# ScalarE normalises half the columns of the first LayerNorm, copies the turned x before the high parts, and takes four copies of the second tokens

## What is computed

```
for i in range(DEPTH):                         # DEPTH = 2
    h = gated_short_conv(x, ...) if i == 0 else chunked_spatial_gating(x, ...)
    x = layer_norm(ALPHA * x + h, ln1_g[i], ln1_b[i])      # the first LayerNorm
    scores = sigmoid(x @ router_w[i])                      # 256 x 64
    # 4 of 8 groups by the sum of their two best scores, then 8 experts in them
    f = sum over the chosen experts: gate * (silu(x @ w_gate[e]) * (x @ w_up[e])) @ w_down[e]
        + the shared expert
    x = layer_norm(ALPHA * x + f, ln2_g[i], ln2_b[i])      # the second LayerNorm
```

## Time and profile before

| | |
|---|---|
| median of 3 runs | 1288.47 us |
| profiled execution, its own time | 1289.11 us |
| its span | 1287.3 us (1.81 us lie around it) |
| PE busy | 1205.8 us, 94% |
| DVE busy | 566.8 us, 44% |
| ACT busy | 376.9 us, 29% |
| POOL busy | 16.2 us, 1% |
| data moved by DMA | 473.87 MB, mean 368 GB/s |

### The profile page before, as it was taken

How to read it: one execution, slowest core, us unless ns; L and a number is a source line. 1 busy time by engine, 2 the same in 40 slices (tenths; PEclk the granted TensorE clock), 3 DMA queues, 4 the chain that set the end, 5 groups by cost and what they waited for, 6 DMA issues and landing times.

```text
span 1287.3 us, 20264 instructions
## 1 busy us (share of the span) xinstructions
PE 1205.8 (94%) x7896; PEld 732.6 (57%) x7896; DVE 566.8 (44%) x1264; ACT 376.9 (29%) x672; POOL 16.2 (1%) x32
## 2 busy tenths in 40 slices
PE   9999999999788888999999999999999898889897
PEld 7986444444234434559999998544444442444454
DVE  5756443333233223327676766634333332332233
ACT  4443221222022222315454444322222220222222
POOL 0001000000000000000000000000000000000000
PEclk9999999999889999999999999999999998999999
DMA  9977999999999999999735435899999999999996
GB/s 302 388 303 314 389 419 416 414 420 421 421 420 422 421 420 421 421 407 401 283 137 194 157 143 238 328 416 416 415 411 421 421 421 420 420 422 420 421 420 260
DMA packets 93937, 473.87 MB, mean 368 GB/s; under 512 B 8336, under 2 KB 23824, under 8 KB 48784
## 3 DMA queue, kind: packets, MB, share of 16 engines
q1 hardware_dynamic: 91776, 469.79, 90.1%
q10 hardware_dynamic: 2064, 2.75, 0.6%
HBM read 471.46 MB, written 1.05 MB: 367 GB/s over the span
## 4 chain that ended last, share of the span: by engine, by line
PE 64%; DMA 25%; SPq 5%; DVE 3%; issue 1%; ACT 1%; POOL 0%; DVEq 0%; ACTq 0%
DMA ring<-in_w_up 24%; PE ps L922 19%; PE ps L794 10%; PE ps L978 7%; PE ps L806 7%; PE ps L844 5%; PE ps L901 4%; PE ps L995 3%; SPq L495 3%; PE ps L934 2%; PE ps L1017 2%; SPq L522 2%; PE ps L1025 1%; PE ps L889 1%; SPq L535 1%
## 5 line engine op out<-in xcount | busy, mean ns | idle before, releaser
L922 PE MATMUL ps<-ring,xsT 128*32 128x512 f32 (+1 forms) x2048 | 328.3, 615 | 50.2 <-DMA ring<-in_w_up 50.0
L922 PEld LDWEIGHTS ps<-ring,xsT 128*32 128x32 f32 (+1 forms) x2048 | 104.6, 124 | 265.1 <-issue 263.6
L1739 DVE SCALAR_TENSOR_TENSOR sig<-sig,slot_gate,ps 128x256 f32<-128x256 f32 x52 | 25.0, 480 | 364.7 <-ACT sig L1374 364.7
L978 PE MATMUL ps<-ring,hidT 128*32 128x512 f32 (+1 forms) x1168 | 182.4, 596 | 2.5 <-DMA ring<-in_w_down 2.1
L1521 DVE TENSOR_TENSOR ring_low<-ring,wh 128x1024 fp32r<-128x1024 f32 (+1 forms) x110 | 126.4, 1149 | 88.0 <-ACT wh L1293 87.1
L1293 ACT CAST wh<-ring 128x1024 fp32r<-128x1024 f32 (+1 forms) x110 | 108.8, 990 | 145.9 <-PE ps L794 61.3
L1762 DVE TENSOR_TENSOR X<-X,ps 128x512 f32<-128x512 f32 x184 | 118.3, 683 | 52.2 <-PE ps L995 37.5
L1374 ACT ACTIVATE sig<-ps 128x256 f32<-128x256 f32 x52 | 20.0, 385 | 402.1 <-PE ps L922 345.5
L1753 DVE TENSOR_TENSOR yl<-ps,yh 128x512 fp32r<-128x512 f32 x104 | 71.6, 691 | 128.8 <-ACT yh L1383 128.8
L1362 ACT ACTIVATE xsT<-ps,cols 128x256 f32<-128x256 f32 x208 | 102.5, 561 | 83.1 <-PE ps L901 83.1
L1383 ACT CAST yh<-ps 128x512 fp32r<-128x512 f32 x104 | 60.6, 587 | 171.4 <-PE ps L978 144.5
(11 more groups left out here) (228 smaller groups left out, 1392.0 us busy)
## 6 DMA issues: line engine op xcount, KB each, us to landing
ring<-in_w_gate SPq DMA_DIRECT2D x124, 1024.0 KB, 20.8
ring<-in_w_up SPq DMA_DIRECT2D x124, 1024.0 KB, 23.6
ring<-in_w_down SPq DMA_DIRECT2D x124, 1024.0 KB, 24.1
ring<-in_b_w_in SPq DMA_DIRECT2D x7, 3072.0 KB, 23.4
ring<-in_b_w_out SPq DMA_DIRECT2D x4, 3072.0 KB, 10.7
ring<-in_a_w_in SPq DMA_DIRECT2D x9, 1024.0 KB, 12.1
ring<-in_w_gate SPq DMA_DIRECT2D x8, 512.0 KB, 24.9
ring<-in_a_w_out SPq DMA_DIRECT2D x1, 3072.0 KB, 18.5
```

Of the source, the lines that this page charges most:

```text
L922: last = nc.tensor.matmul(ps[first:first + width, p, :], xsT[:, c, p * P + first:p * P + first + width], gate_up_of(layer, k, c), start=(c ...
L978: last = nc.tensor.matmul(ps[first:first + width, 4 + h, :], hidT[:, p, kk * P + first:kk * P + first + width], down_of(layer, k)[:, kk, h ...
```

## The change

DVE normalises only columns 0 to 511 of each tile and first writes `shift`, minus the mean times the reciprocal root; ACT normalises columns 512 to 1023 with it (`x_high`), and PE and ACT wait for both. ACT now normalises both tiles' halves before its copies, then makes the eight copies of the first tokens and four of the second tokens' eight, then takes the sigmoids, and only then makes the three high parts and issues the load of the next router matrix. PE has four filling products between the tiles in the place of seven. The second LayerNorm, which had this division before, only changes the names of its semaphores.

```diff
@@ -1004,7 +1004,10 @@
                 s = FILL_SLOT[layer][shared]
 
                 def router(t, chunks):
-                    pe.wait_ge((W.xT_ready, W.xT1_ready)[t], W.past.xT_ready + chunks[-1] // 4 + 1)
+                    if t == 1 and chunks[0] == 0:
+                        pe.wait_ge(W.xT1_ready, W.past.xT1_ready + 1)
+                    else:
+                        pe.wait_ge(W.xT_ready, W.past.xT_ready + t + chunks[-1] // 4 + 1)
                     for c in chunks:
                         last = nc.tensor.matmul(ps[:, 4 + t, 0:E], (xT0s, xT1s)[t][:, c, :], rw[:, c, :],
                                                 start=(c == 0), stop=(c == KC - 1))
...
@@ -1027,9 +1030,11 @@
                     return last
 
                 keep_clock_up(3, 2)
-                transposes(0, W.x_ready, W.past.x_ready, W.xT_done)
-                keep_clock_up(3, 7)
-                transposes(1, W.x_ready, W.past.x_ready, W.xT_done)
+                for t in range(TT):
+                    pe.wait_ge(W.x_high, W.past.x_high + t + 1)
+                    transposes(t, W.x_ready, W.past.x_ready, W.xT_done)
+                    if t == 0:
+                        keep_clock_up(3, 4)
                 pe.wait_ge(g.rw_in, 16 * (layer + 1))
                 for t in range(TT):
                     for half in range(2):
...
@@ -1272,7 +1277,7 @@
                     pe.nop()
                 if layer + 1 < DEPTH:
                     for t in range(TT):
-                        pe.wait_ge(A.x2_high, t + 1)
+                        pe.wait_ge(W.x_high, W.past.x_high + TT + t + 1)
                         transposes(t, W.x2_ready, W.past.x2_ready, A.x2T_done)
                     keep_clock_up(3, 4)
 
...
@@ -1395,20 +1400,32 @@
                         last = scaled(xT0s[:, c, :], ps[:, 4 + half, (c % 4) * P:(c % 4 + 1) * P], layer, c)
                     last.then_inc(W.xT_ready, 1)
 
+                def copy_xT1():
+                    act.wait_ge(W.xT_done, W.past.xT_done + 4)
+                    for c in range(4, KC):
+                        last = scaled(xT1s[:, c, :], ps[:, 7, (c % 4) * P:(c % 4 + 1) * P], layer, c)
+                    last.then_inc(W.xT_ready, 1)
+
                 def copy_high(t, chunks):
                     act.wait_ge(W.x_ready, W.past.x_ready + t + 1)
+                    act.wait_ge(W.x_high, W.past.x_high + t + 1)
                     nc.scalar.copy(xh[:, t, chunks], X[:, t, :].rearrange("p (q c) -> p c q", c=KC)[:, chunks]).then_inc(W.xh_ready, 1)
 
                 nc.scalar.activation(unused[:], minus_half[:], ACT.Sigmoid)
-                copy_high(0, slice(0, KC))
+                for t in range(TT):
+                    act.wait_ge(W.shifted, W.past.shifted + t + 1)
+                    nc.scalar.activation(X[:, t, HALF:D], ps[:, 5 + 2 * t, :], ACT.Identity,
+                                         bias=shift[:, t:t + 1], scale=rstd[:, t:t + 1]).then_inc(W.x_high, 1)
                 act.wait_ge(g.cols_in, 16)
                 copy_xT0(0)
                 copy_xT0(1)
-                copy_high(1, slice(0, KC // 2))
-                copy_high(1, slice(KC // 2, KC))
+                copy_xT1()
                 for t in range(TT):
                     act.wait_ge(W.logits, W.past.logits + t + 1)
                     nc.scalar.activation(score[:, t, :], ps[:, 4 + t, 0:E], ACT.Sigmoid).then_inc(W.scored, 1)
+                copy_high(0, slice(0, KC))
+                copy_high(1, slice(0, KC // 2))
+                copy_high(1, slice(KC // 2, KC))
                 if layer + 1 < DEPTH:
                     act.dma_start(rw[:], router_w[layer + 1].rearrange("(p c) e -> p c e", c=KC)).then_inc(g.rw_in, 16)
 
...
@@ -1486,9 +1503,9 @@
                 if layer + 1 < DEPTH:
 
                     for t in range(TT):
-                        act.wait_ge(A.shifted, t + 1)
+                        act.wait_ge(W.shifted, W.past.shifted + TT + t + 1)
                         nc.scalar.activation(X[:, t, HALF:D], ps[:, SUM_BANKS[t] + 1, :], ACT.Identity,
-                                             bias=shift[:, t:t + 1], scale=rstd[:, t:t + 1]).then_inc(A.x2_high, 1)
+                                             bias=shift[:, t:t + 1], scale=rstd[:, t:t + 1]).then_inc(W.x_high, 1)
                     split_high(1, 1)
                 else:
 
...
@@ -1497,8 +1514,8 @@
                         nc.scalar.activation(bias1_row[:, h * HALF:(h + 1) * HALF], ps[:, SUM_BANKS[1] + h, :], ACT.Identity, scale=-1.0 / D,
                                              accum_out=total[:, h:h + 1]).then_inc(A.settled, 1)
                     act.wait_ge(A.settled, 2)
-                    nc.scalar.activation(shift[:, 1:2], total[:, 0:1], ACT.Identity, bias=total[:, 1:2]).then_inc(A.shifted, 1)
-                    act.wait_ge(A.shifted, TT + 1)
+                    nc.scalar.activation(shift[:, 1:2], total[:, 0:1], ACT.Identity, bias=total[:, 1:2]).then_inc(W.shifted, 1)
+                    act.wait_ge(W.shifted, W.past.shifted + TT + 1)
                     nc.scalar.activation(bias1_row[:],
                                          ps[:, SUM_BANKS[1]:SUM_BANKS[1] + 2, :].rearrange("p a b -> p (a b)"), ACT.Square,
                                          bias=shift[:, 1:2], accum_out=total[:, 3:4]).then_inc(A.settled, 1)
...
@@ -1533,8 +1550,10 @@
 
                 def normalise(t):
                     dve.wait_ge(W.ln_rstd, W.past.ln_rstd + t + 1)
-                    nc.vector.tensor_scalar(X[:, t, :], ps[:, 4 + 2 * t:6 + 2 * t, :].rearrange("p a b -> p (a b)"),
-                                            mv[:, t, 0:1], rstd[:, t:t + 1], ALU.subtract, ALU.mult).then_inc(W.x_ready, 1)
+                    nc.vector.tensor_scalar(shift[:, t:t + 1], mv[:, t, 0:1], rstd[:, t:t + 1], -1.0,
+                                            ALU.mult, ALU.mult).then_inc(W.shifted, 1)
+                    nc.vector.tensor_scalar(X[:, t, 0:HALF], ps[:, 4 + 2 * t, :], mv[:, t, 0:1], rstd[:, t:t + 1],
+                                            ALU.subtract, ALU.mult).then_inc(W.x_ready, 1)
 
                 sums_of(0, 0)
                 step(sums_of(0, 1))
...
@@ -1570,7 +1589,7 @@
                 def normalise(t):
                     dve.wait_ge(W.ln2_rstd, W.past.ln2_rstd + t + 1)
                     nc.vector.tensor_scalar(shift[:, t:t + 1], mv[:, t, 0:1], rstd[:, t:t + 1], -1.0,
-                                            ALU.mult, ALU.mult).then_inc(A.shifted, 1)
+                                            ALU.mult, ALU.mult).then_inc(W.shifted, 1)
                     nc.vector.tensor_scalar(X[:, t, 0:HALF], ps[:, SUM_BANKS[t], :], mv[:, t, 0:1], rstd[:, t:t + 1],
                                             ALU.subtract, ALU.mult).then_inc(W.x2_ready, 1)
 
...
@@ -1589,7 +1608,7 @@
                     statistics(0)
                     centre(0)
                     scale(0)
-                    dve.wait_ge(A.shifted, TT + 1)
+                    dve.wait_ge(W.shifted, W.past.shifted + TT + 1)
                     dve.wait_ge(A.settled, 3)
                     step(nc.vector.scalar_tensor_tensor(X[:, 1, :], sums(1), shift[:, 1:2], gain_row[:], ALU.add, ALU.mult))
                     dve.wait_ge(W.ln2_rstd, W.past.ln2_rstd + 2)
...
@@ -1771,13 +1790,12 @@
 
                 first, second = slice(0, KC // 2), slice(KC // 2, KC)
                 dve.wait_ge(g.cols_in, 16)
-                for half in range(2):
-                    dve.wait_ge(W.xT_done, W.past.xT_done + half + 3)
-                    for c in range(4 * half, 4 * half + 4):
-                        last = nc.vector.tensor_scalar(xT1s[:, c, :], ps[:, 6 + half, (c % 4) * P:(c % 4 + 1) * P],
-                                                       cols[:, 4 * layer, c:c + 1], cols[:, 4 * layer + 1, c:c + 1],
-                                                       ALU.mult, ALU.add)
-                    last.then_inc(W.xT1_ready, 1)
+                dve.wait_ge(W.xT_done, W.past.xT_done + 3)
+                for c in range(4):
+                    last = nc.vector.tensor_scalar(xT1s[:, c, :], ps[:, 6, c * P:(c + 1) * P],
+                                                   cols[:, 4 * layer, c:c + 1], cols[:, 4 * layer + 1, c:c + 1],
+                                                   ALU.mult, ALU.add)
+                last.then_inc(W.xT1_ready, 1)
                 for t in range(TT):
                     dve.wait_ge(W.scored, W.past.scored + t + 1)
                     step(nc.vector.tensor_tensor(biased[:, t, :], score[:, t, :], rb[:, layer, :], ALU.add))
```

(4 more changed lines are left out.)

## The result

The changed kernel takes 1297.54 us (median of 6 runs, 1295.28 to 1298.44) against 1288.35 us (6 runs, 1287.94 to 1289.69). The ratio is 1.0066, with a 95% interval of 1.0054 to 1.0078: 0.7% slower. The profiled execution took 1297.59 us with a span of 1295.9. Two single runs further on, one of e2 (2258.4 us, mean granted clock 0.863) and one of e10 (1405.94 us, 0.811), were in a slow state and stand outside every comparison.

The account below looks back on a forecast made before the run. The first LayerNorm and routing were taken as a serial stretch bounding each layer, with ACT's copies as co-bound. Copies 0.21 plus hold 1.47 make 1.68 a layer, 3.4 for both: 1291.9 us, range 1288.2 to 1295.0.

Parts of the forecast that it names:

- the hold: Choice of experts: DVE's two-operand SBUF instruction waits while POOL's low part reads SBUF; 1.47 us a layer in the likeliest case.
- The divided normalisation and what it meets: First LayerNorm: second tokens' X 0.70 us sooner, but ACT's copies, and so the second sigmoid, 0.21 later.
- no hold: Choice of experts: DVE isn't held by POOL, only 0.21 us a layer remains, 0.4 in all, 1288.9 us; chance 0.35.
- Holding goes both ways and by order of arrival: POOL's low part and DVE's two-operand SBUF instructions: whichever comes first makes the other wait; price between 0 and 2.87 us a layer.
- I take DVE first: Choice of experts: DVE's first two-operand instruction precedes POOL, the next starts 1.47 us late; 1.68 a layer, 3.4 in all; chance 0.37.
- The case that was forecast: DVE ahead of POOL in the choice of experts, holding both ways: 3.4 us for both layers, 1291.9 us; chance 0.37.
- A fall to 1.2 GHz would add a little: PE idle for nearly 3 us in the choice if POOL comes first; a lower clock would add a little, no figure given.
- POOL-first rival: Choice of experts: DVE's first two-operand instruction waits 2.77 us for POOL; 2.98 a layer, 6.0 in all, 1294.4 us; chance 0.23.
- In full to the end, once in each layer: First LayerNorm and routing are a serial stretch: what it gains or loses reaches the kernel's end in full, in each layer.
- The copies of the second tokens, the filling products and the later load: First LayerNorm and routing: divided copies covered by 0.47 us, four products for seven free, router load at about 113.7 delays nobody.

Follow-up runs that it names:

- e2: Changed kernel with POOL's low part held back until DVE's first two-operand instruction is done; ratio 1.0040, four runs from 1292.45 to 1295.16 us against 1288.66.
- e10: Changed kernel with POOL's low part halved, DVE copying all second tokens, ACT's second normalisation half after two copies, six filling products; 1286.9 us against 1288.33.
- e1: Changed kernel with POOL's instruction on the first tokens' low part only writing zeros, that part left out of the result; 1289.05 us against 1288.66, ratio 1.0008.
- e9: Changed kernel with one more small ACT instruction between the second sigmoid and the first tokens' cast; 1290.76 us (one run) against 1288.33.
- e3: Changed kernel with 11 filling products on PE ahead of its wait for the choice; 1295.35 us, ratio 1.0051.
- e5: Kernel before with only the high parts, and the router load behind them, moved behind the two sigmoids; 1298.49 us against 1288.58, ratio 1.0072.
- e8: Kernel before with four filling products between the tiles' transposes in the place of seven, nothing else; 1288.30 us, ratio 0.9999.
- e4: Changed kernel, but ACT casts the first tokens between its two halves of the normalisation; 1289.82 us against 1288.66, ratio 1.0006.

## Why the prediction was wrong

The forecast was 1291.9 with a range up to 1295.0; the time is 1297.54. The direction and the mechanism of the hold were right; the order of the two instructions and the price of the clock were not.

- **The divided normalisation and what it meets** held. The transposes of the second tokens were to start 0.70 sooner and did so by 0.73 (104.00 - 99.51 against 104.36 - 99.14), ACT's copies 0.21 later (measured 0.19), the second sigmoid 0.21 later (0.18). With the hold taken away, e1 comes out at the 0.4 us that the "no hold" rival named, though its interval holds zero as well.
- **Holding goes both ways and by order of arrival** held, and is now shown in both orders: e1, e2, e9. The Trainium skill, "SBUF — State Buffer", section "Who interferes with whom", says this of a VectorE instruction with two SBUF inputs and a GpSimd instruction that reads SBUF; the traces agree with 2.96 us for 0.29 with POOL first, and 1.95 and 1.67 with DVE first.
- **"I take DVE first"** is the first step that failed. POOL came first, by 0.06 us, in both layers. Counted from POOL's first root, L1814 started at 12.51 us and POOL at 12.45, where the sum has 12.54 for both. The difference is mostly the cast: it took 2.04 us behind the sigmoid, and the sum used 2.09, its length in the first LayerNorm before. Two starts that come out equal in a sum of some ten terms are no ground for a choice; two cases 1.3 us a layer apart should have been given as one, with both prices. The case that was forecast exists: e9 ran into it and took 1290.76, 2.4 us over its kernel before, where the forecast was 3.4; e2, with DVE first as well, took 3.8 to 6.5 more. With POOL first the sum was 2.98 a layer, and 0.18 + 2.67 = 2.85 was measured.
- **"A fall to 1.2 GHz would add a little"** is the second, and the larger. The term was 3.14 us in layer 0 of the profiled execution, as much as the hold. In the stretch behind `chosen` the chain of waits is PE's products, and at half the clock 3.14 of about 6.8 us (116.8 to 123.6) were lost. The row cited for it had 0.8 us of idle time; the rival had nearly 3. This is what put the time out of the range: the POOL-first rival's 1294.4, which had no such term, lies between the fastest run and the median of e3 (1293.43 and 1295.35), where PE's wait is filled; with 3.14 added it is 1297.5, and 1297.54 was measured. That this agrees so closely is in part luck, since the sum had the two holds 0.3 too high and neither the 0.37 ahead of the stage nor the 0.6 given back. That the fall hangs on the idle time is argued, not shown: what is shown is that it came in three of the four routings profiled with 2.5 us of idle time (the changed kernel's and e5's), and in none of e2's, e3's and e9's, where the wait was shorter or filled. Which execution gets a fall stays open.
- **In full to the end, once in each layer** held within 0.6 of 9.2 us in the profiled execution.
- **The copies of the second tokens, the filling products and the later load** were costed at nothing. For the products e8 agrees in the kernel before. The load was to be issued at about 113.7; in the profile its issue stands at 109.96, right behind the start of the first cast, so it moved by less than a microsecond. Whether the small gaps left by copies and products together let the clock fall now and then, as in e4 and perhaps in e1's two slower runs, stays open.

## What to carry to other kernels

Before moving an instruction behind a wait, list what every engine does at its new time, not only who waits for it: here a transfer of work with 1.1 us of slack by its waits cost 5.3 us by the operands it reads. In this kernel a POOL instruction that reads SBUF belonged under DVE instructions that read PSUM: L1536 and the copies L1777 took 1.34 and 2.64 us with POOL beside them for a part of each, and the same in e5 without it. And where a serial stretch hangs on PE, price the idle time twice: once as itself, once as the clock that may be gone when it ends.

## What the runs showed of the hardware that was not expected

A difference of 0.09 us in the arrival of two instructions (0.06 ahead in the changed kernel, 0.03 behind in e9) decides which DVE instruction is held, and for 2.67 or 1.38 us. POOL's instruction, held by DVE in turn, lost only 0.10 (2.97 for 2.87, e9). Behind the same idle 2.5 us of PE the clock fell in layer 0 of the changed kernel's profile but not in layer 1, and in both layers of e5's. That is one way in which a kernel with such a gap can have several times about 3 us apart: the changed kernel's runs spread over 3.2 us (1295.28 to 1298.44), those of the kernel before over 1.8 beside them.
